# A two-layer decoder step: gated rows kept in SBUF, padded rows and first loads re-queued, rotation and sums on VectorE

## The chip, the cores and the metric

The kernel runs on one core of a Trainium2 chip. The metric is device time in microseconds (us) of one launch; lower is better. Its engines run side by side, each through its own instruction list in order, and wait for each other on semaphores: TensorE (PE in the profile), VectorE (DVE), ScalarE (ACT), GpSimd (POOL) and SyncE (SP), which here only issues DMAs. SBUF is the on-chip memory, PSUM the banks that TensorE writes.

## What is computed

One step of a decoder with two layers, for a prompt of 512 tokens and 8 x 8 sample tokens (576 rows together), width 2048. Layer 0 is differential attention over a paged cache. Layer 1 is retention with 8 heads:

```python
q, k = rotate(proj_q, pos), rotate(proj_k, pos) * K_DIM ** -0.5     # per head 256 wide
# rotate: [x1*cos - x2*sin, x1*sin + x2*cos]
for each chunk of 128 tokens:
    o = ((q @ k.T) * decay) @ v + (q @ S) * decay_q                  # v: 512 wide
    S = g * S + (k * decay_k).T @ v
y = x + rms_norm((head_rms_norm(o) * silu(gate)) @ w_out_ret)        # w_out_ret: 4096 x 2048
```

The sample tokens bring a state of their own per head (8 batches of 256 x 512), which is read, used, updated and written back.

## The kernel before

Everything is float32. A product is made of three fp32r matmuls: each operand is split into a high part (ScalarE copies it: `WH`, `XH`) and a rest (VectorE subtracts: `WL`, `XL`). `split_w` does that for one weight chunk of 512 rows x 256 columns, and its two lines (ScalarE's L1573, VectorE's L1899) stand ahead of every 8 projection tiles. A tile (`project`) is 6 matmuls of 288 columns. Weights come by SyncE's `load_w` (L1127), issued when the chunk before has been split.

`plan()` writes one list of stages for the whole program, and each engine runs its own part of every stage in that order. In layer 1 the place of a stage is given in tiles: head h's work is put at tile 16 + 64 h + t (`retention_work`, with `put(t, ...)`), between the tiles of the projections: first the last four column blocks of the input projection (128 tiles), then the output projection, 64 tiles for each head's 512 rows. So head h's retention work lies among the output projection of head h-2. From head 1's rows on, each output block is added to `x_rows` by VectorE (`evacuate` with kind "+", L1921, two instructions for each 4 tiles), out of two pairs of PSUM banks in turn: TensorE may run 4 tiles ahead of it.

A head goes like this. SyncE loads q and k (`load_qk`), v (`load_rvn`), the decay tables, the gate rows (`load_g4`) and 8 states. POOL rotates q and k (`rope_`, five operations each). TensorE makes the sample scores (`rs_keys`). `pad_rows` spreads the 64 sample rows of k and v over 128 partitions with eight small DMAs (L1775, L1776), issued by ScalarE, then `rs_mask` on VectorE uses them. Four chunks of `ret_scores`, `ret_out`, `ret_state` and four `rs_state` follow. At the end `ret_norm` scales, TensorE transposes each of the five 128-row pieces back, and `gate` (VectorE, L2248) multiplies it with `rsg`, the SiLU of the gate rows, into `gt`, a buffer with two halves. `store_ret` (ScalarE, L1808) writes the half to HBM, `load_x` (L1133) reads all 512 rows x 576 back into `XL`, and `split_x` (L1573, L1904) makes `XH` and `XL` of them for the output projection. A gate waits until the store before last of its half has landed (`gt_out0`, `gt_out1`).

Between the layers, `norm_between` normalises the rows, and `x_rec` on POOL adds `XH` and `XL` again into four buffers `mix_raw` (four operations, put at tile 104). `x_mix` and `x_mix_split` make from them the operands of a Strassen-like product (`product`), which does most of the input projection of layer 1.

`relay_area` makes an engine wait until all earlier work on the shared SBUF area is done; `pads` clears four buffers.

Of the kernel before, what the change touches and what calls it, by code (L numbers as in the profile page):

```python
# [92 lines left out]
def adds(s):  # L93
# [10 lines left out]
    if k in ("split_w", "split_x", "split_s"):  # L104
        return {"w_hi": 1, "w_lo": 1}
# [18 lines left out]
    if k == "rope":  # L124
        return {"rotated": 1}
# [72 lines left out]
    if k == "store_ret":  # L198
        return {"gt_out%d" % (a["t"] % 2): 16}
# [245 lines left out]
def load_gated_attention(part, after=None):  # L445
    return Stage("load_x", part=part, kt=4 * part, row=4 * part, width=SEQ if part == 3 else T, layer=0, after=after)
# [46 lines left out]
class Products:  # L493
# [35 lines left out]
    def product(self, m):  # L529
# [3 lines left out]
                           freed=self.drains.get(freed), mixed=self.mixes.get(X_OF[i]), opening=m == 0)  # L533
# [41 lines left out]
def retention_work(h, stored):  # L575
# [6 lines left out]
    if h:  # L582
# [3 lines left out]
        for k in range(8):  # L586
            put((-12, 4)[k // 4] + 3 * (k % 4), Stage("load_state", b=2 * (k % 4) + k // 4))
# [38 lines left out]
def layer_one(proj, stored):  # L626

    at = {}
    for h in range(HEADS):
        at = merge(at, {PER_HEAD * h + t: x for t, x in retention_work(h, stored).items()})  # L630
# [5 lines left out]
    for hh in range(2):  # L636
        at = merge(at, turn_values(proj.stores, HEADS - 1, hh, hh, [32 * hh + t for t in (36, 39, 42, 46)]))
    out = []
    for t in range(end + 16):
# [3 lines left out]
        if t < end:  # L643
            out += proj.tile()
    assert not at
# [57 lines left out]
def norm_between(proj, prods):  # L703
# [6 lines left out]
    recs = {buf: Stage("x_rec", q=q, buf=buf) for buf, q in ((3, (1, 1)), (1, (0, 1)), (2, (0, 0)), (4, (1, 0)))}  # L710
    at = {3: lambda: n.transpose(2), 4: lambda: n.square(3), 8: lambda: n.scale(3), 12: lambda: n.square(4), 20: lambda: n.transpose(3),
          24: lambda: n.scale(4), 36: lambda: n.transpose(4), 104: lambda: list(recs.values()),
          54: lambda: prods.load() + prods.load()}
    work = [Stage("x_mix", to=to, half=half, rec=recs[rec]) for to, rec in ((3, 1), (1, 2), (2, 2), (4, 4)) for half in range(2)]
# [1725 lines left out]
```

## Time and profile before

| what | value |
|---|---|
| time, median of 3 runs | 3645.84 us (3644.45 to 3646.31) |
| the profiled execution: its time, its span | 3648.98 us, 3647.2 us |
| busy: PE, VectorE, ScalarE, POOL | 93%, 58%, 31%, 6% of the span |
| mean granted TensorE clock | 0.979 of full |
| DMA | 698.20 MB, mean 191 GB/s |

The span is the time from the first to the last recorded instruction. A busy PE is not PE at its peak, as ends of matmuls are modelled; PE's idle time and the granted clock are therefore read by stretch.

### The profile page before, as it was taken

What the parts mean: (1) busy time and instruction counts of PE and PEld (TensorE: products, weight loads), DVE (VectorE), ACT (ScalarE), POOL (GpSimd) and SP (SyncE); (2) the same over time, 40 slices, a digit from 0 to 9 for tenths busy, and PEclk for the clock granted to TensorE, in tenths of its full rate; (3) what the DMA queues carried; (4) which work ended last, traced back from release to release, by engine and by line L of the source; (5) the groups of instructions that cost most, each with busy time, mean ns of one, the idle gap of its engine ahead of it and who ended that gap; (6) DMA issues with size and microseconds to landing.
All of it is one profiled execution on the core that took longest, in us unless ns stands there. A gap on an engine that the chain in (4) does not pass through costs nothing.

```text
span 3647.2 us, 65439 instructions
## 1 busy us (share of the span) xinstructions
PE 3399.0 (93%) x25284; PEld 2996.4 (82%) x25284; DVE 2123.6 (58%) x3207; ACT 1115.9 (31%) x1646; POOL 232.5 (6%) x171
## 2 busy tenths in 40 slices
PE   7999999999999999887999999999998988888897
PEld 7988887788778777687999999999996767766787
DVE  4467566656656565265666666666653335545565
ACT  4222232222222323133433333333323232222223
POOL 1000000000000000013000000000012111222200
PEclk9999999999999999999999999999999999999999
DMA  5466888888788877635233333333344665556644
GB/s 181 150 210 214 281 270 262 267 272 274 255 271 278 288 259 251 215 139 181 72 114 124 119 112 125 113 119 119 104 159 142 206 209 188 196 208 214 208 138 148
DMA packets 503143, 698.20 MB, mean 191 GB/s; under 512 B 37425, under 2 KB 304818, under 8 KB 499698
## 3 DMA queue, kind: packets, MB, share of 16 engines
q1 hardware_dynamic: 437058, 626.74, 51.9%
q10 hardware_dynamic: 65360, 67.00, 5.4%
q8 instruction: 202, 3.31, 0.4%
q0 software_dynamic: 416, 0.28, 0.1%
q14 instruction: 107, 0.88, 0.1%
HBM read 593.36 MB, written 98.96 MB: 190 GB/s over the span
## 4 chain that ended last, share of the span: by engine, by line
PE 78%; DVE 7%; DMA 5%; issue 3%; ACT 3%; SPq 1%; ACTq 1%; POOL 1%; DVEq 0%; POOLq 0%
PE low_banks L1260 51%; PE high_banks L1260 25%; DMA gated_retention<-area 3%; DVE WL L1899 2%; PE high_banks L1263 2%; DMA area<-in_cache_v 1%; ACT WH L1573 1%; DVE x_rows L1921 1%; DVE area L1995 1%; SPq L1159 1%; ACTq L1776 0%; ACT area L1573 0%; ACTq L1775 0%; DMA WR<-in_w_in_ret 0%; DMA area<-in_cache_k 0%
## 5 line engine op out<-in xcount | busy, mean ns | idle before, releaser
L1260 PE MATMUL low_banks<-XH,WH 128*128 128x288 f32 (+2 forms) x4632 | 1142.0, 314 | 99.7 <-DVE WL L1899 40.1
L1260 PE MATMUL low_banks<-XH,WL 128*128 128x288 f32 (+2 forms) x4632 | 1072.2, 299 | 0.0
L1260 PE MATMUL low_banks<-XL,WH 128*128 128x288 f32 (+2 forms) x4632 | 1072.1, 299 | 0.0
L1260 PEld LDWEIGHTS low_banks<-XH,WH 128*128 128x128 f32 x4632 | 779.7, 193 | 258.8 <-issue 193.9
L1260 PEld LDWEIGHTS low_banks<-XL,WH 128*128 128x128 f32 x4632 | 783.6, 192 | 0.0
L1260 PEld LDWEIGHTS low_banks<-XH,WL 128*128 128x128 f32 x4632 | 781.9, 192 | 0.0
L1260 PE MATMUL high_banks<-area 128*32 128x256 f32 (+8 forms) x4720 | 633.5, 468 | 41.5 <-DMA area<-in_cache_v 14.4
L1899 DVE TENSOR_TENSOR WL<-WR,WH 128x1024 fp32r<-128x1024 f32 x272 | 363.1, 1335 | 226.7 <-ACT WH L1573 220.6
L1260 PEld LDWEIGHTS high_banks<-area 128*32 128x32 f32 (+2 forms) x4720 | 273.9, 139 | 256.8 <-issue 186.1
L1573 ACT ACTIVATE WH<-WR 128x1024 fp32r<-128x1024 f32 x272 | 287.3, 1056 | 630.0 <-PE low_banks L1260 411.4
L1995 DVE STREAM_TRANSPOSE area<-area 128x512 f32<-128x512 f32 x512 | 334.3, 690 | 103.8 <-PE high_banks L1260 61.7
L1573 ACT ACTIVATE area<-high_banks 128x512 f32<-128x512 f32 (+2 forms) x224 | 118.7, 535 | 797.2 <-PE high_banks L1263 441.6
L2135 DVE TENSOR_TENSOR WL<-area,WH 128x1024 fp32r<-128x1024 f32 x187 | 229.2, 1226 | 174.2 <-ACT WH L1573 171.7
L1573 ACT ACTIVATE WH<-area 128x1024 fp32r<-128x1024 f32 x189 | 200.9, 1063 | 232.6 <-DVE area L2129 140.6
L1263 PE MATMUL high_banks<-eye_sb,area 128*128 128x128 f32 (+2 forms) x984 | 158.4, 281 | 82.7 <-DVE area L2248 21.6
L2129 DVE TENSOR_TENSOR area<-area 128x1024 f32<-128x1024 f32 x160 | 196.1, 1225 | 22.6 <-DVE third L2135 1.0
L1263 PEld LDWEIGHTS high_banks<-eye_sb,area 128*128 128x128 f32 (+2 forms) x984 | 116.5, 142 | 102.1 <-issue 73.3
L2351 POOL TENSOR_TENSOR area<-area,power 128x1 f32<-128x1 f32 (+3 forms) x67 | 43.2, 646 | 2320.3 <-DVE area L1870 1772.9
L1260 PE MATMUL high_banks<-mixes,WH 128*128 128x288 f32 x864 | 173.7, 295 | 0.0
L1260 PE MATMUL low_banks<-mixes,WH 128*128 128x288 f32 x848 | 170.5, 295 | 0.0
L2135 DVE TENSOR_TENSOR third<-area,third 128x1024 fp32r<-128x1024 f32 x93 | 114.0, 1226 | 91.9 <-ACT third L1573 91.0
L1630 ACT ACTIVATE area<-low_banks 128x288 f32<-128x288 f32 (+2 forms) x192 | 79.0, 411 | 217.9 <-PE low_banks L1260 207.1
(178 smaller groups left out, 3269.8 us busy)
## 6 DMA issues: line engine op xcount, KB each, us to landing
area<-in_cache_k SPq DMA_DIRECT2D x512, 256.0 KB, 4.8
area<-in_cache_v SPq DMA_DIRECT2D x512, 256.0 KB, 5.2
area<-in_w_in_ret SPq DMA_DIRECT2D x162, 512.0 KB, 5.8
WR<-in_w_in_attn SPq DMA_DIRECT2D x136, 512.0 KB, 5.3
WR<-in_w_out_ret SPq DMA_DIRECT2D x66, 512.0 KB, 3.9
area<-in_state_ret SPq DMA_DIRECT2D x64, 512.0 KB, 7.5
out<-area SPq DMA_DIRECT2D x64, 512.0 KB, 5.0
WR<-in_w_in_ret SPq DMA_DIRECT2D x38, 512.0 KB, 3.8
```

What stands on the lines that cost most here:

```text
L1159: sp.dma_start(Vr[t:128:GROUP, half * GROUP:(half + 1) * GROUP, :], cv[page, :, pair * 512:(pair + 1) * 512].rearrange("a (o j) n -> j (a ...
L1260: return nc.tensor.matmul(out, a, b, start=start, stop=stop, skip_group_check=True)
L1263: return nc.tensor.matmul(out, a, ident[0:n, 0:n], start=True, stop=True, is_transpose=True, skip_group_check=True)
L1573: return nc.scalar.activation(out, in_, ACT.Copy, scale=scale)
L1630: last = nc.scalar.activation(dst[:, lo:hi], bank[2 * cb + b][:, 0:hi - lo], f)
L1899: v.tensor_tensor(WL[:, slot, :, :], WR[:, slot, :, :] if spare is None else spare_chunk[spare], WH[:, slot, :, :].bitcast(f32), SUB).then ...
L1921: last = v.tensor_tensor(dst[:, lo:hi], bank[2 * cb + b][:, 0:hi - lo], dst[:, lo:hi], ADD)
L1995: v.transpose(KTs[:, :, 128 * (u % 2) + 32 * pp:128 * (u % 2) + 32 * pp + 32], Kr[:, slot, :].rearrange("p (m i) -> p m i", i=32)).then_in ...
L2129: v.tensor_tensor(to, a, b, op).then_inc(sem["quad_sums"], 1)
L2135: v.tensor_tensor(lo, quad(r, what), hi.bitcast(f32), SUB).then_inc(sem["w_lo"], 1)
L2351: nc.gpsimd.tensor_tensor(out, a, power[0:R, 0:n], ALU.pow).then_inc(sem[name], 1)
```

## The change

Five edits, all in and ahead of layer 1.

- Gated rows in place: `gate` writes its product into `rsg` itself. `store_ret`, its HBM buffer, the load back and the waits for them go. `split_g` makes `XH` and `XL` straight from `rsg`, at tiles 74 to 86 of the head (91 to 103 for head 0), where `split_x` stood at 97 to 109. Since `rsg` is now held until then, the load of the next gate rows moves from tile 8 to 38, and the SiLU from 22 to 49.
- `pad_rows` is issued by SyncE.
- The rotation is done by VectorE in ten pieces (`rope_` with `part`), one every two tiles from tile -13 to 5.
- `x_rec` is done by VectorE in eight pieces; they and the `x_mix` steps behind them start at tile 77 of `norm_between` instead of 104 and 133 (a tile there is 3 or 6 matmuls).
- At layer 1's start, head 0's q, k and v are loaded behind two weight chunks instead of ahead of them, and its 8 states are spread over tiles 4 to 25 instead of all being queued at once. The first product waits for one pair of projection banks, the second for the other.

```diff
@@ retention_work
     else:
-        put(-8, Stage("load_head"))
-    for which in range(2):
-        put(-13 + which, Stage("rope", which=which))
-    put(8, loads["g"])
-    put(22, Stage("silu_g"))
+        put(-13, Stage("load_head"))
+    for k in range(8):
+        put((-12, 4)[k // 4] + 3 * (k % 4) if h else -12 + 3 * k, Stage("load_state", b=2 * (k % 4) + k // 4))
+    for n in range(10):
+        put(-13 + 2 * n, Stage("rope", which=n // 5, part=n % 5))
+    loads["g"].a["split"] = splits.get(h - 1)
+    put(38, loads["g"])
+    put(49, Stage("silu_g"))
...
-    put(58, Stage("store_ret", t=4))
...
-        put(61 + 3 * t, Stage("store_ret", t=t))
-    kt = CH * (h % 2)
-    put(88 if h == 0 else 82, Stage("load_x", part=h % 2, kt=kt, row=CH * h, width=T, layer=1))
     for k in range(CH):
-        put(97 + 4 * k, Stage("split_x", part=h % 2, kt=kt + k, width=T))
+        splits[h] = Stage("split_g", part=h % 2, k=k, freed=freed)
+        put((74 if h else 91) + 4 * k, splits[h])
@@ norm_between
-    places = [t for t in range(128, 192) if t % 8 in (5, 7)]
+    work = list(recs.values()) + work
+    places = [t for t in range(72, 192) if t % 8 in (5, 7)]
@@ plan
-    opening = {9: [Stage("load_rope")], 4: begun[0] + begun[1], 2: begun[2]}
+    opening = {9: [Stage("load_rope")], 4: begun[0] + begun[1] + [first["q"], first["k"], first["v"]], 2: begun[2]}
...
-    inputs += [Stage("relay_area"), Stage("pads")] + [Stage("load_state", b=2 * (k % 4) + k // 4) for k in range(8)]
+    inputs += [Stage("relay_area"), Stage("pads")]
@@ sync
+            def pad_rows(g):
+                sp.wait_ge(sem["drained5"], c.before("drained5"))
+                sp.wait_ge(sem["kz_ready"], c.before("kz_ready"))
+                for n in ("full4", "full5", "full6", "full7", "rvn_in"):
+                    sp.wait_ge(sem[n], c.before(n))
+                for j in range(4):
+                    rows, padded = slice(16 * j, 16 * j + 16), slice(32 * j, 32 * j + 16)
+                    sp.dma_start(knz[padded, :], kn_s[rows, :]).then_inc(sem["padded_in"], 16)
+                    sp.dma_start(rvz[padded, :], rvn[rows, 4, :]).then_inc(sem["padded_in"], 16)
@@ scalar
+            def split_g(g, part, k, freed):
+                for n in ("drained6", "drained7"):
+                    act.wait_ge(sem[n], c.before(n))
+                act.wait_ge(sem["w_used"], c.after(freed, "w_used"))
+                copy(XH[:, CH * part + k, :], rsg[:, k, :]).then_inc(sem["w_hi"], 1)
@@ vector
+            def split_g(g, part, k, freed):
+                dve.wait_ge(sem["w_hi"], c.done("w_hi"))
+                v.tensor_tensor(XL[:, CH * part + k, :], rsg[:, k, :], XH[:, CH * part + k, :].bitcast(f32), SUB).then_inc(sem["w_lo"], 1)
+            def x_rec(g, q, buf, half):
+                for n in ("x_lo", "y_full"):
+                    dve.wait_ge(sem[n], c.before(n))
+                part = lambda a: a[:, 8 * q[0] + 4 * half:8 * q[0] + 4 * half + 4, HALF * q[1]:HALF * q[1] + HALF].bitcast(f32)
+                v.tensor_tensor(mix_raw[buf][:, 4 * half:4 * half + 4, :], part(XH), part(XL), ADD).then_inc(sem["x_recs"], 1)
+            def rope_(g, which, part):
+                mine = (rqT, rkT)[which]
+                cos, sin = [rope[:, n * T:(n + 1) * T].rearrange("p (o t) -> p o t", o=1) for n in range(2)]
+                if part == 0:
+                    dve.wait_ge(sem["kz_ready"], c.before("kz_ready"))
+                    dve.wait_ge(sem[f"qk_in{which}"], c.before(f"qk_in{which}"))
+                    dve.wait_ge(rope_in, 16)
+                    o.link(v.tensor_tensor(rt[:, 0, :], mine[:, 1, :], sin[:, 0, :], MUL))
+                if part == 1:
+                    o.link(v.tensor_tensor(rt[:, 1, :], mine[:, 0, :], sin[:, 0, :], MUL))
+                if part == 2:
+                    o.link(v.tensor_tensor(mine[:], mine[:], cos.broadcast_to([128, 2, T]), MUL))
+                if part == 3:
+                    o.link(v.tensor_tensor(mine[:, 0, :], mine[:, 0, :], rt[:, 0, :], SUB))
+                if part == 4:
+                    v.tensor_tensor(mine[:, 1, :], mine[:, 1, :], rt[:, 1, :], ADD).then_inc(sem["rotated"], 1)
@@ gate (vector)
-                for m in ("g_ready", f"gt_out{t % 2}"):
-                    dve.wait_ge(sem[m], c.before(m))
+                dve.wait_ge(sem["g_ready"], c.before("g_ready"))
...
-                v.tensor_tensor(to, o4, g4, MUL).then_inc(sem[f"drained{n}"], 1)
+                v.tensor_tensor(g4, o4, g4, MUL).then_inc(sem[f"drained{n}"], 1)
```

The first place is ScalarE's list around the gates of one of the later heads. `area<-area 128x512 x4` is `ret_norm`, `64x256` the copy in `rs_keys`. Before:

```order
L1573 ACTIVATE WH<-WR 128x1024
L1573 ACTIVATE area<-area 128x512 x4
L1808 DMA gated_retention<-area 128x4x64
L1573 ACTIVATE WH<-WR 128x1024
L1808 DMA gated_retention<-area 128x4x128 x2
L1573 ACTIVATE WH<-WR 128x1024
L1808 DMA gated_retention<-area 128x4x128 x2
L1573 ACTIVATE area<-high_banks 64x256
L1775 DMA area<-area 16x256
L1776 DMA area<-area 16x512
L1775 DMA area<-area 16x256
```

And now:

```order
L1580 ACTIVATE WH<-WR 128x1024
L1580 ACTIVATE area<-area 128x512 x4
L1580 ACTIVATE WH<-WR 128x1024 x2
L1580 ACTIVATE area<-high_banks 64x256
L1580 ACTIVATE XH<-area 128x576
L1580 ACTIVATE WH<-WR 128x1024
L1580 ACTIVATE XH<-area 128x576
L1580 ACTIVATE area<-high_banks,area 128x256
```

The five stores and the eight small DMAs have left ScalarE's list, and the copies of `split_g` (`XH<-area`) stand where the padded rows were issued.

The second place is VectorE's list from the end of one head's states to the next head's gates, with the output projection's additions (`x_rows`) between. `high_banks,area` is `gate`. Before:

```order
L1899 TENSOR_TENSOR WL<-WR,WH 128x1024
L1921 TENSOR_TENSOR x_rows<-low_banks,x_rows 128x288 x2
L2248 TENSOR_TENSOR area<-high_banks,area 128x4x64
L1921 TENSOR_TENSOR x_rows<-low_banks,x_rows 128x288 x2
L2248 TENSOR_TENSOR area<-high_banks,area 128x512
L1899 TENSOR_TENSOR WL<-WR,WH 128x1024
L1921 TENSOR_TENSOR x_rows<-low_banks,x_rows 128x288 x2
L2248 TENSOR_TENSOR area<-high_banks,area 128x512
```

And now, where `area<-area 128x576` and `128x1152` are pieces of the rotation:

```order
L1897 TENSOR_TENSOR WL<-WR,WH 128x1024
L2193 TENSOR_TENSOR area<-area 128x576
L1924 TENSOR_TENSOR x_rows<-low_banks,x_rows 128x288 x2
L2195 TENSOR_TENSOR area<-area 128x576
L2273 TENSOR_TENSOR area<-high_banks,area 128x4x64
L2197 TENSOR_TENSOR area<-area 128x1152
L1924 TENSOR_TENSOR x_rows<-low_banks,x_rows 128x288 x2
L2199 TENSOR_TENSOR area<-area 128x576
L2273 TENSOR_TENSOR area<-high_banks,area 128x4x128
L1897 TENSOR_TENSOR WL<-WR,WH 128x1024
L2201 TENSOR_TENSOR area<-area 128x576
L1924 TENSOR_TENSOR x_rows<-low_banks,x_rows 128x288 x2
```

Ahead of each gate, and between a weight split and the additions, a piece of the rotation now stands.

The third place is SyncE's list at the same head's start, with the states (`in_state_ret`) and the weight chunks around. Before:

```order
L1127 DMA WR<-in_w_out_ret 128x4x256
L1227 DMA area<-in_state_ret 128x2x512 x2
L1220 DMA area<-retention_inputs 128x4x576
L1227 DMA area<-in_state_ret 128x2x512
L1127 DMA WR<-in_w_out_ret 128x4x256
L1227 DMA area<-in_state_ret 128x2x512
L1133 DMA XL<-gated_retention 128x4x576
```

And now:

```order
L1123 DMA WR<-in_w_out_ret 128x4x256
L1234 DMA area<-in_state_ret 128x2x512 x3
L1218 DMA area<-area 16x256
L1219 DMA area<-area 16x512
L1218 DMA area<-area 16x256
L1219 DMA area<-area 16x512
L1218 DMA area<-area 16x256
```

In the change six more rows of small DMAs follow, and only then the next weight chunk and the last state; the gate rows and the read of `gated_retention` are gone from here.

## Rows read from the trace of the kernel before

**Rows 1.** page, section 4: shares of the span by line along the chain
```profile
PE low_banks L1260 51%; PE high_banks L1260 25%; DMA gated_retention<-area 3%; DVE WL L1899 2%; PE high_banks L1263 2%; DMA area<-in_cache_v 1%; ACT WH L1573 1%; DVE x_rows L1921 1%; DVE area L1995 1%; SPq L1159 1%; ACTq L1776 0%; ACT area 
```

**Rows 2.** busy by stretch: us, PE, PEld, DVE, ACT, POOL, PEclk, DMA share, GB/s
```profile
2822.60:3509.20 686.60, 610.06 (x3761) 486.43 (x3761) 337.12 (x534) 188.01 (x308) 125.81 (x80) 0.95 0.58 198
```

**Rows 3.** PE's waits in 2822.6 to 3509.2: total us, times, longest
```profile
PE low_banks L1260 <- DVE x_rows L1921: 31.2, 18, 3.7
PE high_banks L1263 <- DVE area L2248: 21.6, 7, 7.0
PE high_banks L1263 <- ACT area L1573: 12.6, 7, 2.5
PE high_banks L1260 <- issue: 6.3, 9, 0.8
```

**Rows 4.** waits from 2300 on: total us, times, longest
```profile
DVE area L2248 <- DMA gated_retention<-area: 99.5, 17, 10.4
```

**Rows 5.** VectorE's timeline at one gate
```profile
3223.31 0.69 DVE L2248 TENSOR_TENSOR area<-high_banks,area 128x512 f32<-128x512 f32 x1 [8.53 <-DMA gated_retention<-area]
```

**Rows 6.** ScalarE's timeline behind that gate
```profile
3239.53 0.53 ACTq L1775 DMA_DIRECT2D area<-area  x1
3245.53 1.06 ACT L1573 ACTIVATE WH<-WR 128x1024 fp32r<-128x1024 f32 x1 [6.03 <-PE low_banks L1260]
```

**Rows 7.** PE's timeline in the same stretch
```profile
3228.94 0.68 PE L1260 MATMUL low_banks<-XH,WH 128*128 128x288 f32 x2
3229.42 0.68 PE L1260 MATMUL low_banks<-XL,WH 128*128 128x288 f32 x2
3230.83 0.42 PE L1260 MATMUL low_banks<-XL,WH 128*128 128x288 f32 x2
3231.09 0.42 PE L1260 MATMUL low_banks<-XH,WL 128*128 128x288 f32 x2
3248.98 0.82 PE L1260 MATMUL low_banks<-XH,WH 128*128 128x288 f32 x2 [3.72 <-DVE x_rows L1921]
```

**Rows 8.** busy time by stretch, around the sums
```profile
1671.00:1684.00 13.00, 8.38 (x57) 7.98 (x55) 11.39 (x4) 3.18 (x3) 12.29 (x3) 0.87 0.23 76
```

**Rows 9.** POOL's timeline there
```profile
1671.71 23.31 POOL L2397 TENSOR_TENSOR area<-XH,XL 128x2304 f32<-128x2304 f32 x4 [12.97 <-DVE XL L2318]
```

**Rows 10.** VectorE's timeline there
```profile
1673.20 22.90 DVE L1899 TENSOR_TENSOR WL<-WR,WH 128x1024 fp32r<-128x1024 f32 x4 [1.57 <-ACT WH L1573]
```

**Rows 11.** SyncE's queue there
```profile
1684.50 9.00 SPq L1186 DMA_DIRECT2D area<-in_w_in_ret  x8
```

**Rows 12.** PE's timeline after it
```profile
1705.09 0.63 PE L1260 MATMUL low_banks<-XH,WH 128*128 128x320 f32 x1 [5.16 <-DVE WL L1899]
```

**Rows 13.** VectorE's groups by shape, 2822.6 to 3509.2: busy, mean ns, idle before
```profile
L1899 DVE TENSOR_TENSOR WL<-WR,WH 128x1024 fp32r<-128x1024 f32 x56 | 80.7, 1441 | 78.8 <-ACT WH L1573 78.5
L1904 DVE TENSOR_TENSOR XL<-XL,XH 128x576 fp32r<-128x576 f32 x28 | 21.2, 758 | 25.3 <-ACT XH L1573 24.9
L1921 DVE TENSOR_TENSOR x_rows<-low_banks,x_rows 128x288 f32<-128x288 f32 x163 | 74.3, 456 | 22.4 <-PE low_banks L1260 18.5
L2235 DVE SCALAR_TENSOR_TENSOR area<-area,high_banks 128x512 f32<-128x512 f32 x112 | 76.2, 743 | 36.1 <-PE high_banks L1260 35.5
```

**Rows 14.** the same groups, 1705 to 1765, POOL idle
```profile
L1899 DVE TENSOR_TENSOR WL<-WR,WH 128x1024 fp32r<-128x1024 f32 x13 | 15.9, 1226 | 35.0 <-ACT WH L1573 34.9
L2161 DVE TENSOR_TENSOR area<-area 128x1152 f32<-128x1152 f32 x8 | 10.9, 1358 | 0.3
```

**Rows 15.** page, section 6, and issues 3205 to 3262: KB each, us to landing
```profile
area<-in_state_ret SPq DMA_DIRECT2D x64, 512.0 KB, 7.5
area<-area ACTq DMA_DIRECT2D x4, 32.0 KB, 4.0
```

**Rows 16.** busy time by stretch, start of layer 1's attention
```profile
2716.90:2756.00 39.10, 32.49 (x206) 31.28 (x207) 11.97 (x15) 6.18 (x9) 19.20 (x10) 0.85 0.59 204
```

**Rows 17.** SyncE's queue there
```profile
2723.32 4.29 SPq L1227 DMA_DIRECT2D area<-in_state_ret  x8
```

More of the change, by code:

```diff
@@ L103, in adds @@
         return {f"gated_in{a['part']}": 16}
-    if k in ("split_w", "split_x", "split_s"):
+    if k in ("split_w", "split_x", "split_g", "split_s"):
         return {"w_hi": 1, "w_lo": 1}
@@ L445, in load_gated_attention @@
 def load_gated_attention(part, after=None):
-    return Stage("load_x", part=part, kt=4 * part, row=4 * part, width=SEQ if part == 3 else T, layer=0, after=after)
+    return Stage("load_x", part=part, kt=4 * part, row=4 * part, width=SEQ if part == 3 else T, after=after)
 def split_gated_attention(part, kt):
@@ L626, in layer_one @@
 def layer_one(proj, stored):
-    at = {}
+    at, splits = {}, {}
+    tiles = [proj.tile() for _ in proj.tiles]
+    users = [t[0] for t in tiles]
     for h in range(HEADS):
-        at = merge(at, {PER_HEAD * h + t: x for t, x in retention_work(h, stored).items()})
+        freed = users[PER_HEAD * h + PER_HEAD - 1 if h > 1 else FILL - 32 + 8 * h + 7]
+        at = merge(at, {PER_HEAD * h + t: x for t, x in retention_work(h, stored, splits, freed).items()})
     last = FILL + PER_HEAD * (HEADS - 1)
@@ L643, in layer_one @@
         if t < end:
-            out += proj.tile()
-    assert not at
+            out += tiles[t]
+    assert not at and len(tiles) == end
     for x in out:
@@ L1127, in load_w, with load_gated @@
                 sp.dma_start(to, weights[w][:, row:row + CH, col:col + 256]).then_inc(sem[f"w_in{slot}"], 16)
-            def load_gated(g, part, kt, row, width, layer, after=None):
-                for n in (("gt_out0", "gt_out1") if layer else ("gated_out", "gs_out")):
+            def load_gated(g, part, kt, row, width, after=None):
+                for n in ("gated_out", "gs_out"):
                     sp.wait_ge(sem[n], c.before(n))
                 sp.wait_ge(sem["w_used"], c.before("w_used") if after is None else c.after(after, "w_used"))
-                sp.dma_start(XL[:, kt:kt + CH, 0:width].bitcast(f32), gated[f"out{layer}"][:, row:row + CH, 0:width]
+                sp.dma_start(XL[:, kt:kt + CH, 0:width].bitcast(f32), gated[:, row:row + CH, 0:width]
                              ).then_inc(sem[f"gated_in{part}"], 16)
@@ L1213, in load_rvn, with load_g4 @@
                 sp.dma_start(rvn[0:SMP, 4, :], values_d[SEQ:T, cols]).then_inc(sem["rvn_in"], 16)
-            def load_g4(g, stored):
+            def pad_rows(g):
[7 more added lines that the diff above has]
+                    sp.dma_start(rvz[padded, :], rvn[rows, 4, :]).then_inc(sem["padded_in"], 16)
+            def load_g4(g, stored, split):
                 wait_stored(stored)
-                for n in ("drained6", "drained7", "kz_ready"):
-                    sp.wait_ge(sem[n], c.before(n))
+                sp.wait_ge(sem["kz_ready"], c.before("kz_ready"))
+                if split is not None:
+                    sp.wait_ge(sem["w_lo"], c.after(split, "w_lo"))
                 row = mixed_row(g, 4)
```

84 lines of the change are left out of this document (23 added, 61 removed).

## Prediction

> **What bounds the kernel now.** I read the chain that ended last first. Half of the span on it is TensorE writing the low banks (projections) and a quarter TensorE on the high banks; among the rest one DMA stands out, the store of the gated rows, with 3% of the span [rows 1]. That is about 110 us, all inside layer 1, in a kernel whose TensorE otherwise decides. So the stretch to read is layer 1, from the first gate store of head 0 to that of head 7: seven heads in 686.6 us, 98.1 us each. TensorE is busy 610.06 us of it, so idle 76.5 us, 10.9 per head, and its mean granted clock is 0.95 [rows 2]. Low clock is time lost too: 5% of 98.1 us is 4.9 us per head, at most, as part of it falls into idle time.
>
> The waits of TensorE in this stretch say for whom: 31.2 us for additions to `x_rows`, 21.6 us for `gate` (both VectorE), 12.6 us for ScalarE, mostly before the gates, and 6.3 us in no wait [rows 3]. VectorE is busy only 337.12 of 686.6 us [rows 2], so it is late, not full. What makes it late is the gate: VectorE waited 99.5 us in 17 gates until a store of `gt` had landed [rows 4], 8.53 us before the gate shown [rows 5]; everything behind it in VectorE's list waits too, the weight split and the additions that free the banks. The second cause is ScalarE: it begins to issue the padded rows at 3239.53 and comes to the weight split only at 3245.53 [rows 6], and TensorE stands 3.72 us until 3248.98 [rows 7]. After such waits the clock is at its lower level (1.2 GHz instead of 2.4): a step of two matmuls takes 0.48 us from 3228.94 to 3229.42, and 0.26 us from 3230.83 to 3231.09 [rows 7].
>
> **The change part by part.**
>
> *Gated rows in place.* No gate waits for a store any more. What hangs on it are the 21.6 us and a large part of the 31.2 us of [rows 3]; the rest of the 31.2 us is the wait behind the padded rows. Together 52.8 us, 7.5 per head. The low clock behind them I put at 4 of the 4.9 us. Gain: 11.5 us per head if nothing takes its place. `split_g` has the work of `split_x` (0.758 us on VectorE, four per head [rows 13]), 23 tiles earlier, where ScalarE used to issue the padded rows; it costs nothing new. Its place in TensorE's order is 26 tiles or more ahead of its use. The gate rows' load moves to tile 38, eleven tiles (8.6 us and more) ahead of the SiLU, among state stores; the read back of the same size is gone, so the DMA engines, at a share of 0.58 [rows 2], have less to do. I cost it at nothing; a late landing would hold ScalarE and through `ret_norm` the gates.
>
> *Padded rows on SyncE.* ScalarE's 6.0 us are free (its gain is inside the 11.5). SyncE now issues eight DMAs, some 5 us at ScalarE's pace, after waiting for `rs_keys`. Behind them stand the next weight chunk and the last state. The chunk is used two chunks later (16 tiles, 12.5 us and more), so 5 us of delay are covered. The state is nearer: it is issued some 5.5 us after the copy of `rs_keys` and takes 7.5 us [rows 15], 13 us together; TensorE comes to `rs_out` 12 tiles after `rs_keys` (9.4 us) with two chunk steps of retention between, which the three extra microseconds have to come from. The pads land 4.0 us after issue [rows 15], so `rs_mask`, eight tiles after `rs_keys` (6.2 us plus a chunk step), may wait a microsecond or two on VectorE. From 0 to 3 us per head; I take 0.5, since TensorE can run 4 tiles past VectorE.
>
> *Rotation on VectorE.* Four pieces of 576 columns and one of 1152, twice: 8 x 0.758 [rows 13] + 2 x 1.358 [rows 14] = 8.8 us per head, 70 us in all. Is there room? Between tile -13 and 7, 20 tiles, TensorE needs 20 x 3 x 0.26 = 15.6 us [rows 7]. VectorE has: rotation 8.8; additions, from head 3 on, 2 x 0.456 every 4 tiles, 4.6; 2.5 weight splits of 1.226 [rows 14], 3.1; five gates of up to 0.69 [rows 5], 3.4. Sum 19.9 us, and it enters the stretch with 4 x 0.743 = 3.0 us of `rs_state` [rows 13]. So it is 7.3 us over, less 3.1 us of bank slack (4 tiles), less 1.8 us that TensorE waits for `ret_norm` anyway (12.6 / 7) and less its transposes for five gates. What is left is 0 to 2.4 us of TensorE time per head. Heads 1 and 2 have no additions and lose nothing. I take 1.0 on average. From below: without POOL's work the weight splits should fall from 1.441 to 1.226 us [rows 13, 14], 1.7 us of VectorE per head, so nothing may be lost.
>
> That fall has to be weighed, for it decides the next part too. While POOL ran the four sums (23.31 us [rows 9]), four weight splits on VectorE took 22.90 us [rows 10], 5.7 each instead of 1.226. Either POOL holds them up, or the loads of that time do. If the first, the slow splits vanish with POOL's work; if the second, they stay. The Trainium skill (SBUF - State Buffer, "Who interferes with whom") says that GpSimd and VectorE share a pair of ports as an exclusive lock, and that a VectorE instruction with two SBUF inputs contends with a GpSimd one that reads SBUF. By that rule the sums term below is the 6 us I take, by the other reading 0.
>
> *Sums on VectorE.* From 1671 to 1684 TensorE is busy 8.38 of 13 us at a clock of 0.87 [rows 8]: 4.6 idle, 1.7 slow, 6.3 us. I take 6. The idle time after 1684 I leave out: there SyncE issues eight large loads for 9.00 us [rows 11], and the weight chunk behind them makes TensorE wait 5.16 us [rows 12]; who comes earlier waits longer. The eight sums cost at most 1.358 us each on VectorE [rows 14], two per chunk, beside one split: 3.9 us in a chunk of some 3.5 us at the dense place (24 matmuls of 320 columns, at 0.13 us for 288 [rows 7]) and 6.2 us later. Bounds: 0 and 12 us.
>
> *First loads.* From 2716.9 to 2756 TensorE is busy 32.49 of 39.1 us, at a clock of 0.85 [rows 16]: 6.6 idle and up to 5.9 slow. SyncE put eight states of 512 KB ahead of the weight chunks [rows 17], and POOL was busy with the rotation 19.20 us [rows 16]. Now the states are spread, and the rotation (8.8 us) fits into 25 tiles (19.5 us), though it can't begin before the clearing of the pads. The first wait (for a chunk split behind that clearing) stays, and a ramp of the clock. I take 8, bounds 3 and 11.
>
> *End.* Head 7's own gates: 2 us, bounds 0 and 4.
>
> Sum: 7 x (11.5 - 0.5 - 1.0) = 70, and 6 + 8 + 2 = 16: 86 us. The profiled execution took 3648.98 us (span 3647.2), so 3563; it lies 3.1 us above the median of 3645.84, against which the forecast is **3560 us**.
>
> **The rivals.**
>
> *A, more comes back.* No lateness on VectorE, the faster splits shorten the way to `ret_norm` too, and 1.5 us more of idle and low clock go: 7 x 13 + 4 + 11 + 6 = 112, 3534 us. For it: VectorE's load without the waits is half the span. Against it: the 12.6 and 6.3 us of [rows 3] have causes that the change doesn't touch. Chance 0.22.
>
> *B, VectorE becomes late by itself.* The sum of 19.9 against 15.6 us above counts no semaphore waits between pieces. If each head loses 6 us more, 7 x 4 + 2 + 8 + 3 = 41, 3605 us. Against it: bank slack and the 14 us of idle time that leave VectorE's list elsewhere in the head. Chance 0.12.
>
> *C, SyncE's padded rows hold up the state or the pads* by their full 3 us per head: 21 us less, 3581 us. Chance 0.10.
>
> *D, slower.* Every rotation piece delays TensorE by its whole length because a split or an addition always stands right behind it: 8.8 us, and with it the low clock stays (4 us) and `rs_keys` waits for the last piece by 3 us, 15.8 per head against the 11.5 gained, and 0.5 for the pads: 34 us lost, less 16 gained elsewhere, 3664 us. It decides once a head loses over 13.8 us. Against it: TensorE's 4 tiles of slack, longer than any piece. Chance 0.03.
>
> *E, no change.* The stall moves from the store to the gate rows' load or the split, with the same length. Chance 0.02.
>
> **How the numbers follow.** The forecast has 0.51, with 3545 to 3580 as its own range. Faster is everything but D and E: 0.95; same 0.02; slower 0.03 (0.2%, 7 us, is about what a measurement of this kernel can tell from no change). The range takes in A and C and reaches towards B: 3527 to 3595.
>
> **What the profile would show.** The chain without `gated_retention`; the seven heads in some 617 us instead of 686.6; TensorE's waits for `gate` under 3 us and for `x_rows` under 15, the clock at 0.99. Weight splits at 1.23 us throughout, also around 1671. Wrong would be: TensorE's waits for `x_rows` or for splits unchanged (B), waits of `rs_out` for `in_state_ret` or of `rs_mask` for the small DMAs (C), splits still slow around 1671 (the sums term), SiLU waiting for its rows (E).

## Result and the profile after

The changed kernel takes **3548.34 us** (median of 4 runs, 3540.97 to 3549.28); the kernel before took 3646.07 us in runs on the same chip. The ratio is 0.9728, 95% interval 0.9711 to 0.9745. The forecast was 3560 us.

The profiled execution has a span of 3547.5 us, 99.7 less than before. First the windows of the seven heads, from the first gate of head 0 to the first gate of head 7, which answers to [rows 2], and TensorE's waits in them, which answer to [rows 3] (`L1924` is the addition to `x_rows`, `L2273` the gate, `L2237` a score mask):

```profile
core 0: us, PE busy (x) PEld busy (x) DVE busy (x) ACT busy (x) POOL busy (x), PEclk, DMA share, GB/s
2810.60:3410.60 600.00, 578.67 (x3757) 462.38 (x3758) 383.34 (x602) 190.07 (x307) 10.94 (x14) 1.00 0.59 198
```

```profile
PE high_banks L1270 <- ACT area L1580: 12.5, 7, 2.5
PE low_banks L1267 <- DVE x_rows L1924: 6.5, 5, 1.3
PE high_banks L1267 <- DVE area L2237: 1.4, 6, 0.2
PE high_banks L1270 <- DVE area L2273: 0.7, 1, 0.7
PE high_banks L1267 <- issue: 0.2, 1, 0.2
```

The seven heads take 600.0 instead of 686.4 us between the same two instructions. TensorE's idle time fell from 76.5 to 21.3 us, and its busy time from 610 to 579 us with the same matmuls: the granted clock is 1.00 instead of 0.95. The waits for the gate (21.6 us) and for `x_rows` (31.2 us) are 0.7 and 6.5 us. VectorE is busier (383 instead of 337 us), and TensorE waits for one of its additions 1.3 us at most.

Between the layers TensorE had three waits for weight splits in the kernel before, one of 3.10 us that ended at 1677.99 and these two (start, duration, engine, line, in brackets the idle time ahead and its releaser):

```profile
1684.04 0.38 PE L1260 MATMUL low_banks<-XH,WH 128*128 128x256 f32 x1 [1.55 <-DVE WL L1899]
1690.09 0.41 PE L1260 MATMUL low_banks<-XH,WH 128*128 128x320 f32 x1 [2.92 <-DVE WL L1899]
```

And the changed kernel there: TensorE, VectorE and SyncE's queue, one timeline each, which answer to [rows 10 to 12]:

```profile
1704.61 0.64 PE L1267 MATMUL low_banks<-XH,WH 128*128 128x320 f32 x1 [10.56 <-DVE WL L1897]
...
1679.41 1.23 DVE L1897 TENSOR_TENSOR WL<-WR,WH 128x1024 fp32r<-128x1024 f32 x1 [1.57 <-ACT WH L1580]
1682.37 1.22 DVE L1897 TENSOR_TENSOR WL<-WR,WH 128x1024 fp32r<-128x1024 f32 x1 [1.74 <-ACT WH L1580]
...
1684.11 8.92 SPq L1182 DMA_DIRECT2D area<-in_w_in_ret  x8
1693.08 66.08 SPq L1123 DMA_DIRECT2D WR<-in_w_in_ret  x14
```

The weight splits take 1.23 us where they took 5.7. The three waits are gone, but the one behind the eight large loads has doubled, from 5.16 to 10.56 us. From the first of these loads to the step that waits for the weight chunk behind them, 20.5 us pass now (1684.11 to 1704.61) and 20.6 passed before (1684.50 to 1705.09); what TensorE does meanwhile has become shorter, so it waits longer.

At the start of layer 1, the timelines of TensorE, ScalarE and SyncE's queue in the changed kernel, and TensorE's first step of the kernel before in the last line:

```profile
2716.87 0.85 PE L1267 MATMUL low_banks<-XH,WH 128*128 128x288 f32 x2 [6.98 <-DVE WL L1897]
...
2714.43 1.06 ACT L1580 ACTIVATE WH<-area 128x1024 fp32r<-128x1024 f32 x1 [10.42 <-DMA WR<-in_w_in_ret]
...
2701.76 0.95 SPq L1200 DMA_DIRECT2D area<-retention_inputs  x2
2702.94 0.36 SPq L1208 DMA_DIRECT2D area<-retention_values  x1
2703.35 0.52 SPq L1209 DMA_DIRECT2D area<-retention_values  x1
2706.80 0.38 SPq L1123 DMA_DIRECT2D WR<-in_w_in_ret  x1
...
2716.92 0.85 PE L1260 MATMUL low_banks<-XH,WH 128*128 128x288 f32 x2 [3.75 <-DVE WL L1899]
```

q, k and v are now issued ahead of the third weight chunk, which lands behind them. By the program ScalarE may split the first chunk only when the third has landed too, as both count on one semaphore. So the first split begins at 2714.43, and TensorE waits 6.98 us for it; before it waited 3.75 us there.

To compare executions, also those of the experiments below, I cut each span at instructions that all the kernels have: TensorE's step behind a wait of 4.11 us for the sums of squares (its start depends on the attention part, which no edit touches: 1613.7 to 1622.1 us), the first product that reads mixed inputs, the first step of layer 1, and the first gates of head 0 and of head 7. All in us, worked out from the timelines:

```
kernel         norm to product  products  head 0  seven heads  end
before              177.8         923.5    105.2     686.4    138.7
changed             168.1         926.9     93.7     600.0    136.9
after_again         168.3         927.2     93.7     599.9    136.9
gate_only           173.9         922.9    101.3     639.2    136.7
pads_only           177.0         923.1    103.1     664.9    138.2
pads_act            169.4         927.1     98.1     642.5    138.5
rope_pool           168.2         926.5    100.0     593.3    136.6
rope_at_once        165.2         927.3    105.2     648.5    136.5
rope_mixed          164.1         927.0     93.7     594.7    137.3
xrec_pool           170.9         926.2     93.9     598.6    136.8
first_old           168.3         924.0     95.5     600.0    136.3
w3_first            168.3         922.9     97.2     599.9    136.7
quads_apart         158.0         927.1     93.7     600.7    136.9
quads_rope          157.0         927.4     93.7     594.5    137.1
```

Only the first column scatters: xrec_pool, rope_at_once and rope_mixed went through the norm 1.6 us and through the first weight chunks 1.5 us faster than the others, with nothing edited there, so they are compared with each other in it. The other columns repeat within about 1 us where nothing was edited. For the changed kernel against before: -9.7 + 3.4 - 11.5 - 86.4 - 1.8 is -106.0 us, and the attention part of this execution was 6.3 us slower: -99.7, the whole difference.

### The profile page after: what moved, and what is told of

The parts are those of the page before. It is cut to its first block and busy times, and to the rows that moved or that the text cites. A ratio compares the mean times of both kernels' runs of the same rounds, so it can differ in the third digit from the quotient of the medians.

```text
span 3547.5 us, 65360 instructions
## 1 busy us (share of the span) xinstructions
PE 3363.6 (95%) x25284; PEld 2969.9 (84%) x25284; DVE 2168.2 (61%) x3295; ACT 1118.4 (32%) x1646; POOL 67.1 (2%) x87
## 5 line engine op out<-in xcount | busy, mean ns | idle before, releaser
L1267 PE MATMUL low_banks<-XH,WH 128*128 128x288 f32 (+2 forms) x4632 | 1127.8, 310 | 61.2 <-DVE WL L1897 31.6
L1267 PEld LDWEIGHTS low_banks<-XH,WH 128*128 128x128 f32 x4632 | 770.5, 190 | 210.7 <-issue 159.5
L1267 PEld LDWEIGHTS low_banks<-XL,WH 128*128 128x128 f32 x4632 | 773.2, 190 | 0.0
L1267 PEld LDWEIGHTS low_banks<-XH,WL 128*128 128x128 f32 x4632 | 773.0, 190 | 0.0
L1897 DVE TENSOR_TENSOR WL<-WR,WH 128x1024 fp32r<-128x1024 f32 x272 | 328.0, 1206 | 152.9 <-ACT WH L1580 147.1
L2132 DVE TENSOR_TENSOR area<-area 128x1024 f32<-128x1024 f32 x160 | 196.1, 1226 | 21.1
L1580 ACT ACTIVATE third<-area 128x1024 fp32r<-128x1024 f32 x93 | 98.9, 1064 | 133.0 <-DVE area L2132 65.5
```

The lines of the kernel that those rows point to most:

```text
L1267: return nc.tensor.matmul(out, a, b, start=start, stop=stop, skip_group_check=True)
L1580: return nc.scalar.activation(out, in_, ACT.Copy, scale=scale)
L1897: v.tensor_tensor(WL[:, slot, :, :], WR[:, slot, :, :] if spare is None else spare_chunk[spare], WH[:, slot, :, :].bitcast(f32), SUB).then ...
L2132: v.tensor_tensor(to, a, b, op).then_inc(sem["quad_sums"], 1)
```

## The experiments

The theory: the trip of the gated rows through DRAM made the waits of the heads, and the low clock came behind them. The rivals to it: the padded rows on ScalarE, or the rotation on GpSimd, had a share of their own. Each experiment has theories and rivals of its own, numbered in the text that was written ahead of it. Ratios are to the kernel before on the same chip.

**after_again**, the changed kernel unaltered.

> The changed kernel once more, beside the others on one chip, as the measure for differences of a few microseconds. Expected 3545 to 3551 us; seven heads 599 to 601 us, TensorE's wait between the layers 10 to 11 us. If the variants of a few microseconds were only differences between executions, this one will lie within 2 us of them.

3546.08 us, ratio 0.9724 (0.9711 to 0.9737). The wait between the layers was 10.73 us. On a chip where the variants below are 16 us faster or 58 slower, this one is where it was.

**gate_only**: the rows gated in place, with the padded rows, the sums and the first loads as before and the rotation back on GpSimd. It is not the first edit alone: the rotation stays in ten pieces two tiles apart, and the first two products keep their separate waits.

```
+ rope, x_rec on nc.gpsimd; pad_rows in act's list; recs whole at tile 104
+ q, k, v at prods.mm[prods.count - 5]; 8 x load_state ahead of layer one
  (kept: gate into rsg, split_g, load_g4 at 38, silu_g at 49, no store_ret, no load_x)
```

> Of the four edits only the first is left: the rows are gated in place and split from there; rotation on GpSimd, the padded rows issued by ScalarE, the sums of the inputs on GpSimd in one piece at tile 104 and the first loads of layer one in the old order. Theory 1 (the first edit alone carries the seven heads): seven heads 600 to 612 us, the stretch between the layers and the start of layer one as before (sum 6.8 + 3 slower than the changed kernel there, first gate 105 us after the last product), whole kernel 3565 to 3578 us. Rival 2 (the four edits carry it together: with pads on ScalarE and rotation on GpSimd the weights are still late in each head): seven heads 620 to 650 us, clock about 0.96, kernel 3585 to 3615 us.

3594.72 us, ratio 0.9851 (0.9833 to 0.9868): rival 2. The seven heads take 639.2 us: 47.2 of the 86.4 us gained. TensorE's waits in them:

```profile
PE low_banks L1258 <- DVE XL L1908: 26.3, 6, 5.1
PE high_banks L1261 <- ACT area L1571: 12.5, 7, 2.5
PE low_banks L1258 <- DVE WL L1898: 2.0, 1, 2.0
```

The waits for the gate and for `x_rows` are gone (0.7 and 0.8 us). A new one of 26.3 us has come, for the rests of the gated rows (`XL`), which `split_g` makes.

**pads_act**: the changed kernel, padded rows issued by ScalarE.

```
- def pad_rows (sp):  sp.dma_start(knz[padded, :], kn_s[rows, :]) ...
+ def pad_rows (act): act.dma_start(knz[padded, :], kn_s[rows, :]) ...
```

> The changed kernel with only the padded rows given back to ScalarE. Theory 1 (the eight DMA issues on ScalarE were the start of the ScalarE wait: weights' high parts came 6 us late, TensorE stood 3.7 us each head and its clock fell): TensorE waits for the area or x_rows over 3 us in most heads, seven heads 615 to 630 us, kernel 3562 to 3578 us. Rival 2 (with the rows gated in place ScalarE has room for the issues and the wait is covered by the chunks ahead): seven heads 598 to 604 us, kernel 3545 to 3552 us. Rival 3 (SyncE's issues delay the padded rows, which the mask waits for, 5.3 us in four waits): VectorE's wait for the padded rows goes to zero and the heads gain up to 3 us.

3589.38 us, ratio 0.9838 (0.9822 to 0.9854): theory 1, and more than it said, 42.5 us in the seven heads. VectorE's wait for the padded rows is gone, as rival 3 had it, but nothing is gained by that. This is the place in one head, ScalarE, VectorE and TensorE:

```profile
3106.95 0.53 ACTq L1772 DMA_DIRECT2D area<-area  x1
...
3111.35 0.61 ACTq L1773 DMA_DIRECT2D area<-area  x1
3112.06 1.06 ACT L1570 ACTIVATE WH<-WR 128x1024 fp32r<-128x1024 f32 x1 [5.14 <-PE low_banks L1257]
3113.15 0.68 ACT L1570 ACTIVATE XH<-area 128x576 fp32r<-128x576 f32 x1
...
3113.22 1.23 DVE L1897 TENSOR_TENSOR WL<-WR,WH 128x1024 fp32r<-128x1024 f32 x1 [4.99 <-ACT WH L1570]
3115.46 0.76 DVE L1907 TENSOR_TENSOR XL<-area,XH 128x576 fp32r<-128x576 f32 x1
...
3116.28 0.53 PE L1257 MATMUL low_banks<-XH,WH 128*128 128x288 f32 x2 [4.29 <-DVE XL L1907]
3116.91 0.64 PE L1257 MATMUL low_banks<-XH,WL 128*128 128x288 f32 x2
```

ScalarE issues eight small copies, from 3106.95 to 3111.96, before it makes the high part of a weight chunk. The profile names TensorE as the releaser of its 5.14 us, but these are the issues. VectorE stands 4.99 us for that, and the next `split_g` comes behind it. `project` waits with `w_lo` for all splits ahead of it in the list, `split_g` too, so TensorE stands 4.29 us; 27.4 us in six such waits in the seven heads. Its busy time is 591.66 instead of 578.67 us with the same matmuls: 13 us of slow clock behind the waits. 42.5 is about 27.4 + 2.0 (a wait for `WL`) + 13.

**pads_only**: the kernel before with only the padded rows moved to SyncE.

> The kernel before with one edit: the padded rows issued by SyncE. The rows still go through DRAM. The first edit alone took 47 us off the seven heads, and giving the padded rows back to ScalarE put 42.5 us on. Theory 1 (two stalls at two places of each head, that add up): seven heads 638 to 648 us, x_rows waits of TensorE under 10 us, its waits for the gate still near 21 us, kernel 3598 to 3608 us. Rival 2 (the padded rows hold ScalarE up only because the splits of the gated rows now lie at the same tile; in the kernel before, where they don't, the move is worth little): seven heads 665 to 685 us, kernel 3625 to 3646 us.

3622.86 us, ratio 0.9935 (0.9914 to 0.9957); the seven heads 664.9 us. That is at the edge of rival 2: 21.5 us gained, where the same move behind the first edit brings 46 (gate_only to rope_pool). TensorE's wait for `x_rows` fell from 31.2 to 16.4 us and that for the gate stayed at 21.1. But VectorE now waits for the padded rows, 20.8 us in six waits, where the changed kernel has 5.3. One of them:

```profile
2952.45 0.74 DVE L2201 TENSOR_SCALAR area<-area 128x256 f32<-128x256 f32 x2 [8.38 <-DMA area<-area]
...
2938.06 0.37 SPq L1230 DMA_DIRECT2D area<-retention_inputs  x1
2938.47 0.55 SPq L1237 DMA_DIRECT2D area<-in_state_ret  x1
2939.82 0.52 SPq L1222 DMA_DIRECT2D area<-area  x1
```

The load of the gate rows (L1230, tile 8) and a state are issued on the same queue just ahead of the copies (L1222). In the changed kernel the gate rows are loaded at tile 38. The eight copies land 7.0 to 8.9 us after their issue here; at the same place of the changed kernel (2912 to 2924) it is 1.8 to 2.9 us. So the first edit also makes room for the second. That this load is what delays the copies was not tried by itself, and the waits for the gates, which stay here, may hide a part of the gain.

**rope_pool**: the changed kernel, rotation on GpSimd.

> The changed kernel with only the rotation given back to GpSimd, in the same ten pieces. Theory 1 (the trip of the gated rows through DRAM made the waits; where the rotation runs matters little): the seven heads stay at 600 to 606 us gate to gate, the splits of the weights on VectorE rise from 1.22 to about 1.35 us each (56 x 0.13 = 7 us of VectorE time that is mostly idle time's), x_rows waits of TensorE in the seven heads at or below the 6.5 us of now, whole kernel 3546 to 3556 us. Rival 2 (GpSimd's rotation was a cause of its own: the splits beside it come late and TensorE's clock falls with them): splits back at 1.44 us, the seven heads at 612 us or more, clock under 0.98 in them, kernel 3560 to 3575 us. Rival 3 (ten pieces on VectorE made VectorE late, so taking them off gains): seven heads 594 to 597 us, kernel 3542 us.

3545.03 us, ratio 0.9717 (0.97 to 0.9733), the same as the changed kernel; but no theory had its parts. The seven heads are 6.7 us faster (593.3 us, a little more than rival 3 said), and head 0 is 6.3 us slower, on one wait; its place on TensorE, and the rotation that it waits for on GpSimd:

```profile
2741.98 0.56 PE L1267 MATMUL high_banks<-area 128*64 128x64 f32 x4 [5.05 <-POOL area L2415]
...
2722.03 2.28 POOL L2407 TENSOR_TENSOR area<-area 128x576 f32<-128x576 f32 x1 [1060.24 <-DVE area L2184]
2740.54 1.39 POOL L2415 TENSOR_TENSOR area<-area 128x576 f32<-128x576 f32 x1
```

The weight splits are 1.40 us in the mean (1.22 in the changed kernel), between theory 1's 1.35 and rival 2's 1.44, and cost nothing in the seven heads.

**rope_mixed**: head 0 on VectorE, heads 1 to 7 on GpSimd.

```
  def rope_ (dve):  + if g > 0: return
  def rope_ (pool): + if g == 0: return
```

> The changed kernel with the rotation of head 0 on VectorE as changed and that of heads 1 to 7 on GpSimd, ten pieces each. With the rotation wholly on GpSimd the seven heads took 593.3 us instead of 600.0, and the way from the first step of layer one to the first gate 100.0 instead of 93.7 us, with a TensorE wait of 5.05 us for GpSimd's rotation of head 0. Theory 1 (two effects of opposite sign that cancelled: lateness of VectorE in seven heads, GpSimd's slow rotation on the path of head 0): first step to first gate 93 to 95 us, seven heads 592 to 595 us, kernel 3538 to 3544 us. Rival 2 (the differences are those between executions): both stretches as in the changed kernel, kernel 3547 to 3550 us.

3538.34 us, ratio 0.9695 (0.9676 to 0.9713). Head 0 93.7 us, the seven heads 594.7: theory 1. Two effects had cancelled. (In this execution the norm was 4 us faster too, see the table.)

**rope_at_once**: the ten pieces not spaced.

```
- put(-13 + 2 * n, Stage("rope", which=n // 5, part=n % 5))
+ put(-13 + n // 5, Stage("rope", which=n // 5, part=n % 5))
```

> The changed kernel with the five pieces of q's rotation at one tile and the five of k's at the next, instead of two tiles apart: VectorE then does 4.4 us and 4.4 us with little between. Theory 1 (TensorE can run four tiles, 3.1 us, past VectorE; a block of 8.8 us is longer than that): TensorE waits 3 to 6 us more per head for the additions to x_rows or for a weight split, its clock falls behind the wait, seven heads 620 to 650 us, kernel 3568 to 3600 us. Rival 2 (additions to x_rows and splits find room before and behind it): seven heads 598 to 606 us, kernel within 5 us of the changed one.

3603.72 us, ratio 0.9886 (0.9871 to 0.9901): theory 1 for the seven heads (648.5 us), and 4 us more than it gave the kernel. The spacing is worth 58 us against after_again, more than half of what the whole change brought. TensorE's waits in its seven heads:

```profile
PE low_banks L1267 <- DVE x_rows L1924: 37.1, 5, 7.4
PE high_banks L1270 <- ACT area L1580: 12.4, 7, 2.5
PE high_banks L1270 <- DVE area L2273: 9.7, 2, 6.7
```

Head 0, of which the theory said nothing, is 11.5 us slower for the same reason: a weight split stands behind its own block (TensorE waits 3.74 us), and its first gate behind the block of head 1 (6.73 us).

**xrec_pool**: the changed kernel, the four sums on GpSimd at tile 104.

> The changed kernel with the four sums of the inputs given back to GpSimd, whole and at tile 104, the rest as changed. Theory 1 (VectorE and GpSimd hold each other up: splits of 5.7 us beside sums of 5.8 us): the splits of the weights beside the sums take over 4 us again, TensorE waits some 8 us there at a clock of 0.87, but a part of the 10.6 us wait behind the first loads of the quads is then hidden by it; net 4 to 8 us slower, 3553 to 3557 us. Rival 2 (the gain of 6.8 us in that stretch came from elsewhere, or the wait behind the quads takes all of it up): within 2 us of the changed kernel, 3547 to 3551 us, with the splits slow all the same.

3549.51 us, ratio 0.9734 (0.9718 to 0.9751). That is the time that rival 2 gave, but the kernel's time can't tell 3 us from none. The stretch can: 170.9 us against 164.1 and 165.2 in executions of its kind, 5.7 to 6.8 us slower, as theory 1 had it. GpSimd and VectorE there:

```profile
1672.31 23.29 POOL L2415 TENSOR_TENSOR area<-XH,XL 128x2304 f32<-128x2304 f32 x4 [11.46 <-DVE XL L2336]
...
1673.80 22.89 DVE L1896 TENSOR_TENSOR WL<-WR,WH 128x1024 fp32r<-128x1024 f32 x4 [1.57 <-ACT WH L1579]
```

gate_only against the changed kernel gives 5.8 us for the same thing. gate_only against before gives 3.9 us more for something that I had not costed: `proj1_drained` is now waited for at the second product, not the first, and the wait of 2.33 us for `third` ahead of the products is gone with it. Which of the two made it is not separated.

**first_old** and **w3_first**: the first loads in the old order; q, k, v behind the third chunk.

```
first_old: - opening {4: begun[0] + begun[1] + [q, k, v]}   + q, k, v at mm[count - 5]; states ahead of layer one
w3_first:  + opening {4: begun[0] + begun[1], 2: begun[2] + [q, k, v]}
```

> The changed kernel with only the order of the first loads given back: q, k and v of head 0 issued before the two weight chunks, and the eight states at the end of the inputs' products. Theory 1 (the reorder gains by the states out of the chunks' way and loses by the third chunk behind q, k, v): TensorE's wait at the first step of layer one falls from 7.0 to about 3.7 us, then the first chunks come late, first step to first gate 99 to 105 us instead of 93.7; kernel 3550 to 3557 us. Rival 2 (without GpSimd's rotation the order does not matter): first step to first gate 93 to 95 us, kernel 3545 to 3548 us.

3543.57 us, ratio 0.971 (0.969 to 0.973).

> The changed kernel with q, k and v of head 0 issued behind the third weight chunk instead of ahead of it. Theory 1 (the third chunk lands late behind q, k, v and is what TensorE waits 7.0 us for at the first step of layer one): that wait falls to 3 to 4 us, nothing is lost later, since the rotation of head 0 begins only after the clearing of the pads; kernel 3543 to 3547 us. Rival 2 (q and k become late for the rotation, or the wait is for a split behind other work on VectorE): wait at the first step unchanged or moved to the keys of head 0, kernel 3548 to 3552 us.

3542.86 us, ratio 0.9705 (0.9686 to 0.9723). Neither can be told from the changed kernel, and neither theory 1 came as it stood. Products and head 0 together take 1020.6 us in the changed kernel, 1019.5 and 1020.1 here. In first_old the first wait is 4.15 instead of 6.98 us, and head 0 1.8 us longer. In w3_first it is 3.13 us, and a new one of 4.79 us follows, for the split behind the clearing of the pads, which begins after 8.10 us of idle time on VectorE: in the program it stands behind a step (`relay_area`) at which all loads must have landed, q, k and v with them. The wait has moved, as rival 2 had it.

**quads_apart**: the quads' first loads one by one.

```
- 54: lambda: prods.load() + prods.load()
+ at_quads = {54 + 8 * i: [x] for i, x in enumerate(prods.load() + prods.load())}
```

> The changed kernel with the eight first loads of the quads issued one by one, eight tiles apart from tile 54 on, instead of all at once at tile 54. Theory 1 (the weight chunk queued behind the eight loads is what TensorE waits 10.6 us for between the layers): that wait falls to under 2 us, the whole kernel 3538 to 3543 us, if no later chunk waits behind a quad. Rival 2 (the DMA engines are full there and the wait only spreads over several chunks, or moves to the first product, which needs the quads' sums): the waits of this stretch add up to 8 us or more as now, kernel 3546 to 3550 us.

3534.05 us, ratio 0.968 (0.9661 to 0.9698): theory 1, and some 4 us better than it said. The stretch is 10.1 us shorter, and no wait of 1 us or more is left in it behind 1672. SyncE's queue: weight chunks and quads alternate. Behind the burst of the changed kernel the next chunk is issued at 1693.08 and lands 9.0 us later; the one issued at 1687.46 here lands after 4.6 us.

```profile
1684.37 0.37 SPq L1125 DMA_DIRECT2D WR<-in_w_in_ret  x1
1684.85 0.43 SPq L1184 DMA_DIRECT2D area<-in_w_in_ret  x1
1687.46 0.37 SPq L1125 DMA_DIRECT2D WR<-in_w_in_ret  x1
```

**quads_rope**: quads_apart and rope_mixed together.

> The changed kernel with the quads' first loads one by one, eight tiles apart, and the rotation of heads 1 to 7 on GpSimd. Theory 1 (the two gains, 14 and 10 us against the changed kernel, lie in different stretches and add up): kernel 3524 to 3530 us, first step to first gate 93 to 95 us, seven heads 593 to 596 us. Rival 2 (part of either was the difference between two chips, some 4 us each): 3530 to 3536 us.

**3530.04 us**, ratio 0.968 (0.9667 to 0.9694), 16.0 us below after_again on the same chip; the stretches give 11.3 + 5.4 = 16.7. It is the fastest of all, between the two expectations. That quads_apart was 14 and rope_mixed 10 us below the changed kernel was in part the difference between executions. Its seven heads:

```profile
2799.10:3393.60 594.50, 578.43 (x3757) 462.52 (x3758) 338.35 (x534) 190.19 (x307) 136.23 (x80) 1.00 0.60 201
```

## Why the prediction was right, point by point

The time (3548.3 against 3560) and the sign of each term were right. The largest term was too small, and the first loads were right in size in part for another reason than given. By stretches the edits brought 106.0 us where the sum said 86; that the time came as near as 12 us is in part luck, as far as the profiled executions show: the attention part, which no edit touches, was 6.3 us slower in the changed kernel's.

- *What bounds the kernel*: right. The waits for the gate and for `x_rows` went, and the low clock with them.
- *Seven heads, 70 us*: 86.4. Per head 12.3 instead of 10.0. The idle time fell by 7.9 us per head (55.2 / 7), where 7.5 less 0.5 and 1.0 was said: the waits without a releaser (6.3 us) and for `WL` (4.1 us) of before went too, 1.5 per head. The sum had left them out; it is the step that was mis-sized. The clock gave 4.5 (610 less 579 us busy, / 7), where 4 was said. And the padded rows cost nothing where 0.5 was said.
- *Rows gated in place*: the gross gain of 11.5 measured 13.3 ((686.4 - 593.3) / 7, with the rotation on GpSimd). It is 6.7 by the first edit (gate_only, with the rotation's spacing on GpSimd, which was not tried alone) and 6.6 by the padded rows (gate_only to rope_pool, with the sums and first loads, which lie elsewhere). The two don't simply add: in the kernel before, the padded rows' move brings 3.1 (pads_only). The text put ScalarE's part "inside the 11.5" and gave it no number; it is half. `split_g` "costs nothing new" was right only because the padded rows left ScalarE: at the same tile the two together cost 6.1 us per head (pads_act).
- *Padded rows on SyncE, 0.5*: 0 as far as the waits show. The mask waits 5.3 us on VectorE in the seven heads (3.9 before), and no wait of TensorE is put down to it. Rival C, the full 3 us, did not come. (Of the eight copies per head, three follow behind the five that the change's list of SyncE shows, not six.)
- *VectorE's lateness, 1.0*: 6.7 / 7 = 0.96 us, by rope_pool. The pieces' prices held (0.76 and 1.36 us). Rival B is what happens without the spacing: 6.9 us more per head (rope_at_once), near B's 6; two tiles apart it does not come. Rival D, every piece delaying TensorE by its whole length, did not come in either. The "from below" of the text, that faster splits pay for it, did not come: the splits were 1.22 instead of 1.40 us, and the 0.96 us were lost all the same.
- *Sums on VectorE, 6*: 5.7 to 6.8. The reading by the lock (the Trainium skill, SBUF - State Buffer, "Who interferes with whom") agrees with the trace: splits of 1.23 us without GpSimd's sums, 5.7 with them, whatever the loads do. The splits at 1685.47 and 1688.68 of the changed kernel, amid the eight large loads, took 1.23 us too. Each by itself, splits and sums ran by turns, as the last section shows. The stretch gained 9.7, with 3.9 from around the first product, which I had not costed.
- *First loads, 8*: 8.1 (11.5 less 3.4), in part by another cause. The order of the loads, which gave the term its name, brought nothing (first_old). Given back alone, the rotation, which the text had named too, costs head 0 6.3 us (rope_pool) and the padded rows 4.4 (pads_act); given back together, with the old loads, they cost 7.6 (gate_only), so the two overlap. The other 3.9 us lie between gate_only and the kernel before. The third chunk behind q, k and v, which costs the 3.4, was not in the prediction: I had counted the queue ahead of the moved states, not behind the moved loads.
- *End, 2*: 1.8; no run was made to find its cause.
- *Rival A* had 13 us per head where the forecast had 10; 12.3 lies nearer to A, and so do the 106.0 us by stretches (A had 112). One of A's three reasons came: 1.5 us more of idle time per head, against which the text had set the 6.3 us without a releaser, and these did go. The other two did not: the lateness stayed, and so did the 12.5 us ahead of the gates, although the splits were faster. Nor did A's higher values of the first loads (11) and the end (4).

## What to carry to other kernels

Two edits that each remove a wait may need each other: here ScalarE's copies cost 6 us per head when `split_g` stood at the same tile, and moving them to SyncE in the kernel before, with its other loads and waits, was worth only 3. Work that is moved to a busy in-order engine should go in pieces shorter than the slack of the engine that waits for it; the same ten instructions cost 1 us per head spaced and 8 in a block. And when a stretch gets faster, look at the loads issued by program order in it. Their transfer took as long as before, so here the burst of large loads ahead of a needed chunk turned a part of the gain into a wait, until it was spread.

## What the runs showed of the hardware

- Short waits cost more than their length. Six waits of about 4.5 us in 642 us (pads_act) stand beside 13 us more busy time of the same 3757 matmuls, at a granted clock of 0.98 instead of 1.00. Behind the wait until 3116.28 a step of two takes 0.48 us (3117.34 to 3117.82), the lower level of 1.2 GHz, where it took 0.27 ahead (3110.51 to 3110.78).
- A weight split on VectorE and an addition on GpSimd ran by turns. In the kernel before, the first sum of 2304 columns, which began ahead of the splits, took 5.14 us, the three behind it 6.1 each; the splits beside them took 4.73 us and three times 6.02, against 1.23 alone, and each ended 1.1 us behind a sum. In rope_pool the 16 pieces of 576 columns on GpSimd that began during a split took 2.27 to 2.42 us, and the other 48 took 1.39 to 1.45, also where a split began behind them or additions to `x_rows` ran beside them. A split took up to 3.4 us, beside a piece of 1152 columns.
- SyncE issued eight loads of 512 KB back to back in 8.92 us: the first four in 0.43 to 0.53 us each, the others in 1.19 to 2.55. With a weight chunk and some 3 to 4 us between them each took 0.43 to 0.55 us (quads_apart). But eight states of the same size, also back to back, took 4.29 us in all [rows 17]; what makes the difference was not tried.
